# Latent attention: square roots and key scaling moved by one step, the queries' rotation cut in two, one weight split taken earlier

## What is computed

```python
c_q, c_kv, k_rope = split(h @ w_in, [256, 512])
q = (rmsnorm(c_q) @ w_q_up).reshape(B, S, 8, 192)
kv = (rmsnorm(c_kv) @ w_kv_up).reshape(B, S, 8, 256);  k_nope, v = split(kv, [128])
k = concat([k_nope, broadcast(k_rope)])
q, k = rope_tail(rmsnorm(q)), rope_tail(rmsnorm(k))   # the last 64 of 192 channels are rotated
o = causal softmax attention of q, k, v
y = o.reshape(B, S, 1024) @ w_out
```

## Time and profile before

| | us |
|---|---|
| median of 3 runs | 1552.59 |
| lowest and highest run | 1550.44, 1556.13 |
| the profiled execution, its own time | 1548.01 |
| its span, first to last instruction | 1546.7 |
| PE busy | 1407.2 (91%) |
| DVE busy | 865.0 (56%) |
| ACT busy | 681.5 (44%) |

### The profile page before, as it was taken

One profiled execution on the slowest core, in us unless ns is written; L12 is line 12 of the kernel. 1 busy time (PEld: TensorE's weight loads), 2 busy tenths in 40 slices (PEclk: granted clock), 3 DMA queues, 4 the chain that ended last, 5 costly groups with the idle time before them and its releaser, 6 DMA issues.

```text
span 1546.7 us, 27421 instructions
## 1 busy us (share of the span) xinstructions
PE 1407.2 (91%) x11609; PEld 1189.8 (77%) x11609; DVE 865.0 (56%) x1546; ACT 681.5 (44%) x1185; POOL 10.6 (1%) x10
## 2 busy tenths in 40 slices
PE   7999999999989868768777799999999998899998
PEld 6999899899966434334343489999999986699997
DVE  6786463475522211212111478988988777588775
ACT  6544554544442111111110466565555566465553
POOL 1000000000000000000000100000000000000000
PEclk9999999999989997998998899999999999999999
DMA  7454354468799999999999744335565342446551
GB/s 239 146 171 148 120 172 132 155 224 326 297 412 424 426 424 422 425 426 425 426 426 425 283 153 134 109 126 193 173 207 182 108 150 74 145 149 206 191 178 68
DMA packets 170641, 372.05 MB, mean 241 GB/s; under 512 B 6912, under 2 KB 137088, under 8 KB 145936
## 3 DMA queue, kind: packets, MB, share of 16 engines
q1 hardware_dynamic: 170512, 370.22, 64.5%
HBM read 369.15 MB, written 1.05 MB: 239 GB/s over the span
## 4 chain that ended last, share of the span: by engine, by line
PE 63%; DMA 22%; DVE 7%; ACT 4%; issue 2%; SPq 1%; DVEq 0%; ACTq 0%
DMA wu<-in_expert_w_down_dram 17%; PE bank L602 16%; PE bank L603 16%; PE bank L604 16%; PE bank L1724 3%; DVE lo L566 2%; PE bank L1696 2%; DMA wu<-in_expert_w_up_dram 2%; PE bank L833 2%; PE bank L1762 2%; ACT hi L555 2%; PE bank L1776 1%; SPq L1295 1%; DMA raw<-in_w_in_dram 1%; PE bank L942 1%
## 5 line engine op out<-in xcount | busy, mean ns | idle before, releaser
L566 DVE TENSOR_TENSOR lo<-raw,hi 128x1024 fp32r<-128x1024 f32 (+2 forms) x315 | 376.4, 1216 | 175.6 <-ACT hi L555 174.7
L602 PE MATMUL bank<-XH,hi 128*128 128x256 f32 x1416 | 404.8, 286 | 7.4 <-DVE lo L566 3.7
L604 PE MATMUL bank<-XH,lo 128*128 128x256 f32 x1416 | 399.8, 282 | 0.0
L603 PE MATMUL bank<-XL,hi 128*128 128x256 f32 x1416 | 399.8, 282 | 0.0
L555 ACT ACTIVATE hi<-raw 128x1024 fp32r<-128x1024 f32 (+2 forms) x315 | 321.3, 1049 | 116.6 <-PE bank L604 68.1
L602 PEld LDWEIGHTS bank<-XH,hi 128*128 128x128 f32 x1416 | 270.4, 191 | 15.8 <-issue 11.5
L603 PEld LDWEIGHTS bank<-XL,hi 128*128 128x128 f32 x1416 | 270.5, 191 | 0.8
L604 PEld LDWEIGHTS bank<-XH,lo 128*128 128x128 f32 x1416 | 270.4, 191 | 0.0
L1724 PE MATMUL bank<-wu,xg 128*32 128x256 f32 x2048 | 166.1, 427 | 50.0 <-DMA wu<-in_expert_w_up_dram 46.8
L1724 PEld LDWEIGHTS bank<-wu,xg 128*32 128x32 f32 x2048 | 70.3, 119 | 122.7 <-DMA wu<-in_expert_w_up_dram 64.1
L1762 PE MATMUL bank<-wu,hidT 128*32 128x256 f32 x1024 | 74.5, 411 | 37.4 <-DMA wu<-in_expert_w_down_dram 26.7
(11 more groups left out here) (383 smaller groups left out, 2175.3 us busy)
## 6 DMA issues: line engine op xcount, KB each, us to landing
wu<-in_expert_w_gate_dram SPq DMA_DIRECT2D x64, 1024.0 KB, 26.6
wu<-in_expert_w_up_dram SPq DMA_DIRECT2D x64, 1024.0 KB, 26.3
wu<-in_expert_w_down_dram SPq DMA_DIRECT2D x64, 1024.0 KB, 26.9
raw<-in_w_in_dram SPq DMA_DIRECT2D x44, 1024.0 KB, 5.2
raw<-in_ffn_w_up_dram SPq DMA_DIRECT2D x44, 1024.0 KB, 5.0
raw<-in_ffn_w_down_dram SPq DMA_DIRECT2D x22, 1024.0 KB, 5.1
raw<-in_hgrn_w_in_dram SPq DMA_DIRECT2D x16, 1024.0 KB, 5.4
raw<-in_w_branch_ret_dram SPq DMA_DIRECT2D x8, 1024.0 KB, 7.2
```

The source lines that it names most:

```text
L566: dve.tensor_tensor(lo_of(u), v, hi_of(u), ALU.subtract).then_inc(*WL.inc(u))
L602: pe.matmul(dst, first[0], first[1], start=start, stop=False)
L603: pe.matmul(dst, second[0], second[1], start=False, stop=False)
L604: return pe.matmul(dst, third[0], third[1], start=False, stop=stop)
```

## The change

The DVE list: `rope` on the queries leaves `q_scale` and becomes `q_turn(i, c)`, which rotates two heads and is called four times: (0,0) and (0,1) back to back where group 0 was rotated, (1,0) in step 2 behind score(1), (1,1) in step 5. A wait on the previous half guards the four scratch tiles `ra`. `k_scale(1)` and the rest of `q_scale(1)` go from step 3 to step 4, behind score(3) and ahead of `normalize(3)`. The first output unit O0 is split on DVE in step 3, ahead of `normalize(2)`. The ACT list: the two roots of group 1 go from step 3 (ahead of the exponentials of head 2) to step 4 (behind `attend(0)`, ahead of the exponentials of head 3), and of the units O1 and O2, which step 4 split, O2 goes to step 5. PE: `turn_q(h)` waits for its own half of the rotation.

```diff
-        O_HI = (0, 0, 1, 1, 3, 4, 5, 6, 7, 7, 9, 10, 11, 12, 13)
-        O_LO = (0, 0, 0, 0, 1, 3, 4, 5, 6, 7, 7, 9, 11, 11, 12)
+        O_HI = (0, 0, 1, 1, 2, 4, 5, 6, 7, 7, 9, 10, 11, 12, 13)
+        O_LO = (0, 0, 0, 1, 1, 3, 4, 5, 6, 7, 7, 9, 11, 11, 12)
...
-                pe.wait_ge(*X.dve.got("rope", "q", h // 4, 1))
+                pe.wait_ge(*X.dve.got("rope", "q", (h // 4, h % 4 // 2), 1))
...
                 if n == 3:
                     turn_p(0)
-                    k_scale(1)
-                    q_scale(1)
                 if 4 <= n < 7 or 9 <= n < 13:
                     turn_p(n - 3 if n < 7 else n - 5)
                 if 4 <= n < 8 or 10 <= n < 14:
                     attend(n - 4 if n < 8 else n - 6)
+                if n == 4:
+                    k_scale(1)
+                    q_scale(1)
...
+            def q_turn(i, c):
+
+                x = Qt[:, :, 4 * i + 2 * c:4 * i + 2 * c + 2, P:192]
+                dve.wait_ge(*X.dve.got("sq", sq_heads("q", i, c, 1) + 1))
+                if (i, c) == (0, 0):
+                    dve.wait_ge(*X.dve.got("rope", "k", (0, 0), 1))
+                else:
+                    dve.wait_ge(*X.dve.got("rope", "q", (i, 0) if c else (i - 1, 1), 1))
+                rope(x, 0, x, 2, "q", (i, c))
+
             def q_scale(i):
                 hs = slice(4 * i, 4 * i + 4)
-                x = Qt[:, :, hs, P:192]
-                dve.wait_ge(*X.dve.got("sq", sq_heads("q", i, 1, 1) + 1))
-                rope(x, 0, x, 4, "q", i)
...
             q_up(0)
-            dve.wait_ge(*X.dve.got("rope", "k", 0, 1))
+            q_turn(0, 0)
+            q_turn(0, 1)
             q_scale(0)
...
+                if n == 2:
+                    q_turn(1, 0)
                 if n in (1, 2):
                     q_up(1, [n - 1])
-                if n == 3:
+                if n == 4:
                     k_scale(1)
-                if n >= 4:
+                    q_scale(1)
+                if n == 5:
+                    q_turn(1, 1)
+                if n >= 3:
                     dve_split(unit2(O_TILE) + O_LO[n])
                 if 1 <= n < 5 or 7 <= n < 11:
                     normalize(n - 1 if n < 5 else n - 3)
-                if n == 3:
-                    dve.wait_ge(*X.dve.got("rope", "q", 0, 1))
-                    q_scale(1)
```

More of the change, by code:

```diff
@@ L3177, in dve_mla @@
             dve.wait_ge(*ANG2.dve.got("trig", 1, 3))
-            rope(kr[:, :, :].rearrange("p t (o n) -> p t o n", o=1), 1, krot[:, :, :].rearrange("p t (o n) -> p t o n", o=1), 1, "k", 0)
+            rope(kr[:, :, :].rearrange("p t (o n) -> p t o n", o=1), 1, krot[:, :, :].rearrange("p t (o n) -> p t o n", o=1), 1, "k", (0, 0))
             dve_split(unit2(Q_TILE[0]) + 2)
```

## The result

| | before | after |
|---|---|---|
| median, 20 runs each (us) | 1553.15 | 1547.91 |
| lowest and highest | 1550.02, 1560.24 | 1544.26, 1553.68 |
| span of the profiled execution | 1546.7 | 1543.3 |

The ratio after to before is 0.9966, 95% interval 0.9956 to 0.9977: 5.2 us, clear of no change though only 0.34%. The forecast was 1547.6 and 5.0. For the profiled execution it was 1543.0, and that took 1544.61, 1.6 more; the next paragraph has the reason.

The account below looks back on a forecast made before the run. PE's waits around the edit bound its entry into a PE-paced stretch. turn_q(4) 5.0 us earlier, including the 0.7 rotation loss and out(0)'s lost clock, takes the median from 1552.6 to 1547.6; range 1543 to 1552.5.

Parts of the forecast that it names:

- What bounds: PE idles around the edit at 1281 to 1302 us; from 1308.4 PE's own pace bounds, so an earlier entry moves its end.
- B - A: Measures from DVE's start of group 0's rotation: A to PE's turn_q(4), B to PE's turns of H behind out(7).
- The rotation in two halves: DVE's query rotation: 1.34 us per half, 0.6 more for group 0 on the path, score(2) 0.7 late.
- Roots behind head 0's result: ACT's chain from the exponentials of head 2: without a break, turn_q(4) at 1303.37 instead of 1308.40, 5.0 us earlier.
- O0 split sooner: DVE's lo of O0 ahead of normalize(2): out(0) starts at 1296.5 instead of 1301.84, at full clock.
- The new gap: PE ahead of turn_q(4): the two old gaps (5.7 us) become one of about 2.0, waiting for ACT until 1303.37.
- The transfer of O4 and O5: Its DMA issues at 1303.1 instead of 1305.50, data at 1307.9; PE does not wait before score(5), cover 0.6 us.
- Rival C: The transfer for O4 and O5 replaces the removed wait; a 3 us delay leaves a gain of 2.6: 1550.0; chance 0.08.
- Rival B: ACT's table loads cost more than their rows, each switch twice as long: gain 2.4 us, 1550.2; chance 0.03.
- Rival A: The new gap ahead of turn_q(4) lowers the clock, costing 1.7 us: gain 3.3, 1549.3; chance 0.30.
- E: Rival: half rotations at their lower bound and no low clock from 1346: gain 7.6 us, 1545.0; chance 0.12.
- D: Rival: a long low-clock stretch behind the new gap covers out(1) and out(2), costing 5.2 us: 1552.8; chance 0.05.

## Why the prediction was right

**What bounds.** Right: B - A stays within 0.3 us of 40.7 in all seven executions in which out(7)'s wait was left alone and the clock fell once, for about four us, behind turn_q(4). The second stretch is PE's pace, and the gain at its entry arrives at its end.

**The rotation in two halves.** Forecast 1.34 each and 0.6 on the path; measured 1.33 to 1.45, and 0.67 by undoing it. The straight line between one head and four was the right price.

**Roots behind head 0's result.** The chain held step by step: exponentials of head 2 at 1294.65 - 1.95 = 1292.70 (forecast 1292.7), turn_q(4) at 1303.23 (1303.37). What the step's name suggests is not what the runs show, though: with the roots early A is only 1.1 larger, so everything else in the change gives 4.1 of the 5.2 without them. Of that, the `lo` of O0 alone gives 1.7. That the rest is DVE's key scaling and rotation moved out of the way of head 3 is argued from the wait of 4.41 us, not shown: no run moved these alone, and none undid the later `hi` of O2 or the halves of group 1.

**O0 split sooner.** out(0) at 1296.46 (1296.5). Undone, it takes 4.9 of the 5.2 back, 2.4 of it by the clock; alone, it gives 1.7. The parts are not additive: out(0), ACT's chain and DVE's chain each come next when another is shortened.

**The new gap.** Forecast about 2.0 and ended by ACT; it is 1.71 and is. Its cause, the two splits on ACT, was shown by moving them.

**The transfer of O4 and O5.** Its issue at 1304.97 - 1.95 = 1303.02 (1303.1), the split at 1307.94 (1307.9), score(4) on DVE at 1312.64 - 1.95 = 1310.69 (1310.7). ACT waits 3.54 us and PE none, as costed. Rival C did not happen.

**Table loads.** Rival B did not happen: the root starts 1.29 after its load, the exponential 1.29 after the other. The Trainium skill (ScalarE: Activation LUTs, What ACT_TABLE_LOAD costs) adds about 1380 ns of drain to every switch. No drain shows with ACT at work without a break either: by the page's figure A would be about 31.0, an estimate, and it is 28.2.

**The clock.** Here the working was incomplete, and in the first profile the number came right by luck. The prediction named a clock below 1 after 1303 as a sign of being wrong, and in the first profile it came: 0.57 in the four us from 1307. Rival A took such a stretch as 1.7 off the gain. The gain over the stage was still 5.0, since the later low stretch of the kernel before, from 1346, then stayed away; the prediction had that only in E, and named no case with both. In the two further executions it was as the sum had it: full clock behind the new gap, and a low stretch behind the wait ahead of out(7). The gain in B is 5.0 and 5.1 there. I had counted the low stretches gap by gap; over the stage the kernel before shows two and the changed one one, the one saved being that around out(0), which the sum did hold. D and E did not happen.

**The whole.** 5.0 forecast; 4.97 in B, 5.2 in the medians. The interval of the ratio allows 3.6 to 6.8 us, so that the medians come within 0.3 of the forecast is luck too; that the steps inside the trace come within 0.3 is not. The upper end of the range, 1552.5, is 0.5 above what its own working gives (C plus 2 is 1552.0), without effect.

## What to carry to other kernels

When several in-order engines feed each other, lay out the chain of each from the trace's start-to-start times, and take the latest at each meeting point: that gave the new bound, its length and its cover to 0.3 us here, which the size of the removed waits (5.7) did not. Look at what stands in an engine's list right in front of the instruction that ends a gap: work due much later (here the splits of O2, O3 and O7) is worth trying at a later place, or an earlier one where a transfer hangs on it; here this gave 6.8 us in B, 1.6 of that by the clock, beside the 5.0 of the change itself. For effects below the spread of the whole, compare within the trace from an instruction that both kernels share.

## What the runs showed of the hardware that was not expected

With the same instructions ahead of it, the rotation of group 0 starts at 1276.97, 1277.18 and 1284.20 in three executions of the changed kernel: 7 us of spread from earlier stages alone, more than the change, while A differs by 0.03. And the same gap of PE of 1.71 us was followed by four us at a granted clock of 0.57 in one of these executions and by full clock in the other two.
